# Conditioning rows of a two-block kernel: computed beside the input projection instead of beside the down projection

## The reference

```python
    u = h @ w_in[l]                                   # first block, 60 tiles of 128 columns
    c_q, c_kv, k_r, u_pool, z, xbc, dt, lru_g, lru_x, gates = jnp.split(u, pts, axis=-1)
    y_a = mla_mixer(c_q, c_kv, k_r, cos, sin, ...)    # attention over latents of u
    ...
    x = x + jnp.square(jax.nn.relu(h2 @ w_ff1[l])) @ w_ff2[l]     # up and down projection
...
    mod = (jax.nn.silu(c) @ w_ada[i] + b_ada[i]).reshape(B, N_ADA, D)[:, :, None, :]
    mod_c = (jax.nn.silu(c_ctx) @ w_ada[i] + b_ada[i]).reshape(N_ADA, D)
    hc = _rmsnorm(ctx, norm1_w[i]) * (1.0 + mod_c[1]) + mod_c[0]
    h = _rmsnorm(x, norm1_w[i]) * (1.0 + mod[:, 1]) + mod[:, 0]
```

## Time and profile before

| what | value |
|---|---|
| device time, median of 3 runs | 3533.78 us (3532.81 to 3534.66) |
| device time of the profiled execution | 3534.49 us |
| its span in the profile | 3532.7 us |
| mean granted TensorE clock | 0.987 |
| PE busy | 3403.0 us, 96% |
| DVE busy | 2259.5 us, 64% |
| ACT busy | 1575.2 us, 45% |
| POOL busy | 799.2 us, 23% |
| HBM read, written | 520.67 MB, 103.19 MB |

### The profile page before, as it was taken

The page is one execution under the profiler, slowest core; times in us unless marked ns, Lnnn a source line. Parts: engine busy times, 40 slices in busy tenths (PEclk is TensorE's granted clock), DMA queues, the critical chain, the costliest instruction groups (busy, mean ns, idle before and its releaser), DMA issues.

```text
span 3532.7 us, 43926 instructions
## 1 busy us (share of the span) xinstructions
PE 3403.0 (96%) x17289; PEld 2803.6 (79%) x17289; DVE 2259.5 (64%) x2915; ACT 1575.2 (45%) x1946; POOL 799.2 (23%) x396
## 2 busy tenths in 40 slices
PE   7999999999999999999999999999896999999998
PEld 6667767667878878888888877777775999999997
DVE  4333445645447675666764854545756899999998
ACT  4344443234322343332213433433545677777776
POOL 3111111112212345544431221111222011101112
PEclk9999999999999999999999999999998999999999
DMA  5111113223465323336542241232633999999998
GB/s 201 49 48 54 66 54 103 78 96 131 160 216 184 101 87 117 117 137 223 203 158 71 81 158 65 81 119 98 191 124 151 389 379 378 388 385 385 380 379 311
DMA packets 131725, 626.75 MB, mean 177 GB/s; under 512 B 14849, under 2 KB 15241, under 8 KB 106690
## 3 DMA queue, kind: packets, MB, share of 16 engines
q1 hardware_dynamic: 126626, 606.12, 46.1%
q0 software_dynamic: 4752, 17.30, 1.8%
q10 hardware_dynamic: 144, 0.52, 0.0%
HBM read 520.67 MB, written 103.19 MB: 177 GB/s over the span
## 4 chain that ended last, share of the span: by engine, by line
PE 55%; DVE 6%; ACT 1%; issue 1%; DMA 1%; POOL 0%; POOLq 0%; DVEq 0%; SPq 0%; ACTq 0%
PE bank L268 8%; PE bank L270 7%; PE bank L269 7%; PE bank L3870 5%; PE bank L3869 5%; PE bank L3868 5%; PE bank L2123 3%; PE bank L2125 3%; PE bank L2124 3%; PE bank L3884 2%; PE bank L3885 2%; PE bank L3886 2%; DVE gqJ L2975 1%; PE bank L3855 1%; PE bank L2849 1%
## 5 line engine op out<-in xcount | busy, mean ns | idle before, releaser
L257 POOL TENSOR_TENSOR WL<-WR,WH 128x1024 fp32r<-128x1024 f32 (+1 forms) x177 | 400.6, 2263 | 1721.6 <-ACT WH L249 1718.5
L268 PE MATMUL bank<-XH,WH 128*128 128x512 f32 x1584 | 637.5, 402 | 10.0 <-ACT stg L553 5.0
L270 PE MATMUL bank<-XH,WL 128*128 128x512 f32 x1584 | 617.9, 390 | 0.0
L269 PE MATMUL bank<-XL,WH 128*128 128x512 f32 x1584 | 617.6, 390 | 0.0
L249 ACT ACTIVATE WH<-WR 128x1024 fp32r<-128x1024 f32 (+1 forms) x177 | 173.4, 979 | 511.4 <-PE bank L270 506.3
L3804 DVE TENSOR_TENSOR EL<-ER,EH 128x2816 fp32r<-128x2816 f32 x120 | 371.3, 3100 | 2.2 <-POOL warm L4095 2.2
L268 PEld LDWEIGHTS bank<-XH,WH 128*128 128x128 f32 x1584 | 297.8, 188 | 88.7 <-issue 15.9
L3799 ACT ACTIVATE EH<-ER 128x2816 fp32r<-128x2816 f32 x120 | 307.5, 2563 | 117.2 <-PE bank L3870 84.4
L269 PEld LDWEIGHTS bank<-XL,WH 128*128 128x128 f32 x1584 | 298.1, 188 | 64.7 <-issue 5.0
L270 PEld LDWEIGHTS bank<-XH,WL 128*128 128x128 f32 x1584 | 297.7, 188 | 62.9
L3868 PE MATMUL bank<-EH,WH 128*128 128x352 f32 x1024 | 336.2, 328 | 1.9 <-DVE WL L3992 1.9
(11 more groups left out here) (655 smaller groups left out, 6956.5 us busy)
## 6 DMA issues: line engine op xcount, KB each, us to landing
ER<-in_wu_dram SPq DMA_DIRECT2D x48, 1408.0 KB, 8.6
ER<-in_wd_dram SPq DMA_DIRECT2D x40, 1408.0 KB, 10.9
WR<-in_w_in_dram SPq DMA_DIRECT2D x89, 512.0 KB, 4.4
ER<-in_wg_dram SPq DMA_DIRECT2D x32, 1408.0 KB, 8.5
WR<-in_w_ff_dram SPq DMA_DIRECT2D x64, 512.0 KB, 4.7
aq<-in_w_ada_dram SPq DMA_DIRECT2D x48, 512.0 KB, 3.6
res<-in_wg_dram SPq DMA_DIRECT2D x16, 1408.0 KB, 8.0
res<-in_wu_dram SPq DMA_DIRECT2D x16, 1408.0 KB, 8.3
```

The source lines that it names most:

```text
L257: e.tensor_tensor(lo, raw, hi.bitcast(F32), ALU.subtract).then_inc(*w_lo.up("w_lo", n))
L268: e.matmul(bank[bk][:, 0:b - a], whi, xhi, start=k == 0, stop=False)
L269: e.matmul(bank[bk][:, 0:b - a], whi, xlo, start=False, stop=False)
L270: mm = e.matmul(bank[bk][:, 0:b - a], wlo, xhi, start=False, stop=k == K - 1)
```

## The change

The 48 rows are loaded and reduced between tiles 0 and 5 of the input projection and in the attention's beginning. The diagonals and the broadcast are made right after tile 0, ACT copies the broadcast from PSUM to SBUF (into buffers that the attention uses later), and each row is reduced in whole rows of 1024 with both operands in SBUF. Rows 16 to 47, which the context doesn't need, are done for the latent vector only, so there are 64 such instructions. Rows 0 to 37 rotate through three buffers, rows 38 to 47 through four.

```diff
+    ADA_EARLY, ADA_CHAIN, ADA_LATE = ((0, 3), (3, 7), (7, 11), (11, 15), (15, 22)), ((22, 25), (25, 29), (29, 32)), 38
...
+    def ada_load(e, a):
+        if a >= ADA_LATE + 4:
+            e.wait_ge(*on("ada.ev", a - 4, 0))
+        elif a >= ADA_LATE:
+            e.wait_ge(*(on("mla.qr", 1, 1, 1) if a == ADA_LATE else on("mla.kr")))
+        elif a >= 3:
+            e.wait_ge(*on("ada.ev", a - 3, 1 if a - 3 < 16 else 0))
+        e.dma_start(ada_raw(a), I["w_ada"][a]).then_inc(*d_ada[ada_slot(a)].up("ada", a))
...
+    def ada_pe(e):
+        for i in range(2):
+            e.wait_ge(*on("ada.diag", i))
+            for h in range(2):
+                e.wait_ge(*on.bank(4 + 2 * i + h, "ada.b", i, h))
+                for k in range(4):
+                    o = i * T + (4 * h + k) * 128
+                    mm = e.matmul(bank[4 + 2 * i + h][:, k * 128:k * 128 + 128], ones, ada_diag[:, o:o + 128],
+                                  start=True, stop=True)
+                mm.then_inc(*mla_pe.up("ada.bc", i, h))
+
+    def ada_act(e):
+        for i in range(12, 16):
+            e.wait_ge(*on("p.out", i))
+        for i in range(2):
+            for h in range(2):
+                e.wait_ge(*on("ada.bc", i, h))
+                e.activation(ada_b[i][:, half(h)], bank[4 + 2 * i + h][:, :], AF.Copy).then_inc(
+                    *mla_act.up("ada.b", i, h))
+
+    def ada_diag_dve(e):
+        e.wait_ge(*on("a0.cv"))
+        for i in range(2):
+            for k in range(8):
+                o = i * T + k * 128
+                e.tensor_scalar(ada_diag[:, o:o + 128], ident, cf[:, 2 * k + i:2 * k + i + 1], None,
+                                ALU.mult).then_inc(*mla_dve.up("ada.diag", i))
+
+    def ada_rows(e, a, b):
+        for x in range(a, b):
+            e.wait_ge(*on("ada", x))
+            for i in range(2 if x < 16 else 1):
...
+                e.wait_ge(*mla_dve.now)
+                e.tensor_tensor_reduce(ada_junk, ada_raw(x), ada_b[i], 1.0, pr("b_ada", x), ALU.mult, ALU.add,
+                                       mod[:, x, i:i + 1]).then_inc(*mla_dve.up("ada.ev", x, i))
@@ attention_sp
+        ada_loads(e, 0, 3)
+        for k, (a, b) in enumerate(ADA_EARLY):
+            st.upto("ada", k)
+            ada_loads(e, a + 3, b + 3)
         st.upto("a0")
...
+        st.upto("mla", "ang")
+        ada_loads(e, 25, 28)
+        st.upto("mla", "q")
+        ada_loads(e, 28, 32)
+        st.upto("mla", "kv")
+        ada_loads(e, 32, 39)
+        st.upto("mla", "rope")
+        ada_loads(e, 39, 48)
@@ attention_pe
+        for k in range(5):
+            st.until(2 * k + 2, "ada", k)
+            if k == 0:
+                ada_pe(e)
         st.until(12, "a0")
@@ attention_act, attention_proj_act
+        e.wait_ge(*on("ada.ev", ADA_LATE - 1, 0))
...
+        if i == 0:
+            e.wait_ge(*on("ada.end"))
@@ attention_dve
+        ada_diag_dve(e)
         e.wait_ge(*on("mla.pos_in"))
...
+        for k, (a, b) in enumerate(ADA_EARLY):
+            st.upto("ada", k)
+            ada_rows(e, a, b)
         st.upto("a0")
...
+            ada_rows(e, *ADA_CHAIN[s])
...
+        ada_rows(e, *ADA_CHAIN[2])
...
+                    if n + h < 2:
+                        a = ADA_CHAIN[2][1] + 3 * g + 2 * n + h
+                        ada_rows(e, a, a + 1)
...
+        ada_rows(e, ADA_LATE, 48)
+        on.at["ada.end",] = mla_dve.now
@@ ff_pe_, ff_dve_, ff_sp
-                            mm = e.matmul(bank[4 + 2 * i + h][:, k * 128:k * 128 + 128], ones, (ac2, acq)[i][:, o:o + 128],
...
-                for i in a[2 * h:2 * h + 2]:
-                    ada_dve(e, i)
...
-            for a in ada_of(t):
-                if a + 2 < 48:
-                    ada_load(e, a + 2)
```

More of the change, by code:

```diff
@@ L623, in program, with ada_slot, ada_raw @@
     mla_pe, mla_act, mla_dve = sem("pe_mla"), sem("act_mla"), sem("dve_mla")
+    ADA_EARLY, ADA_CHAIN, ADA_LATE = ((0, 3), (3, 7), (7, 11), (11, 15), (15, 22)), ((22, 25), (25, 29), (29, 32)), 38
+    d_ada = [dma_sem("ada0"), dma_sem("ada1"), d_p, *d_x]
+    ada_b, ada_junk, ada_diag = (qk[:, 3 * T:4 * T], qk[:, 0:T]), qk[:, 2 * T:3 * T], mcs
+    def ada_slot(a):
+        return a % 3 if a < ADA_LATE else 3 + (a - ADA_LATE) % 4
+    def ada_raw(a):
+        return (*(vN[:, k * T:k * T + T] for k in (1, 2, 3)), PT[:, 0:T], tA, cosT, sinT)[ada_slot(a)]
@@ new lines, in ada_load, with ada_loads @@
+    def ada_load(e, a):
[6 more added lines that the diff above has]
+        e.dma_start(ada_raw(a), I["w_ada"][a]).then_inc(*d_ada[ada_slot(a)].up("ada", a))
+    def ada_loads(e, a, b):
+        for x in range(a, b):
+            ada_load(e, x)
+    def ada_pe(e):
[8 more added lines that the diff above has]
+                mm.then_inc(*mla_pe.up("ada.bc", i, h))
@@ new lines, in ada_rows @@
+    def ada_rows(e, a, b):
+        for x in range(a, b):
+            e.wait_ge(*on("ada", x))
+            for i in range(2 if x < 16 else 1):
+                if x == 0:
+                    for k in range(12, 16):
+                        e.wait_ge(*on("p.out", k))
+                    for h in range(2):
+                        e.wait_ge(*on("ada.b", i, h))
+                e.wait_ge(*mla_dve.now)
+                e.tensor_tensor_reduce(ada_junk, ada_raw(x), ada_b[i], 1.0, pr("b_ada", x), ALU.mult, ALU.add,
+                                       mod[:, x, i:i + 1]).then_inc(*mla_dve.up("ada.ev", x, i))
@@ L638, in attention_sp @@
         e.dma_start(D_dt, cqv[32:40, 5 * T:6 * T]).then_inc(*d_dt.up("dt_out"))
-        for x in ("ang", "q", "kv", "rope", "v"):
-            st.upto("mla", x)
+        st.upto("mla", "ang")
[6 more added lines that the diff above has]
+        ada_loads(e, 39, 48)
+        st.upto("mla", "v")
         e.wait_ge(*on("dt_out"))
@@ L761, in attention_act @@
     def attention_act(e, st):
+        st.upto("ada", 0)
+        ada_act(e)
         st.upto("a0")
@@ L1557, in program @@
     d_xin = [dma_sem(f"x_in{i}") for i in range(2)]
-    d_ada = [dma_sem(f"ada{i}") for i in range(2)]
     d_ret = [{x: dma_sem(f"ret{i}{x}") for x in ("q", "qs", "k", "ks", "v", "g")} for i in range(2)]
@@ L2057, in down_at @@
         return range(8 * q + 8 + 2 * m, 8 * q + 10 + 2 * m) if q < 3 and m < 4 else ()
-    def ada_of(t):
-        return range((t - 2) * 48 // 22, (t - 1) * 48 // 22) if 2 <= t < 24 else range(0)
     def up_store(e, n, b):
@@ L2095, in ff_sp @@
             up_store(e, 15, b)
-        for a in range(2):
-            ada_load(e, a)
         for t in range(32):
@@ L2131, in ff_pe_ @@
             q, m = divmod(t, 8)
[L2132 to L2138, removed]
-                            mm = e.matmul(bank[4 + 2 * i + h][:, k * 128:k * 128 + 128], ones, (ac2, acq)[i][:, o:o + 128],
-                                          start=True, stop=True)
-                        mm.then_inc(*ff_pe.up("ada.bc", i, h))
             for h in range(2):
@@ L2262, in ff_dve_ @@
             relu(3)
[L2263 to L2267, removed]
         for t in range(32):
             q, m = divmod(t, 8)
-            a = list(ada_of(t))
             for h in range(2):
-                for i in a[2 * h:2 * h + 2]:
-                    ada_dve(e, i)
                 rs = xc(m)[:, half(h)]
@@ L2285, in ff_dve_ @@
                                    ALU.mult).then_inc(*V.up("cs"))
[L2287 to L2299, removed]
     def ff_pool_(e):
```

3 lines of the change are left out of this document (removed).

## The result

| | before | with the change |
|---|---|---|
| device time, median | 3534.21 us (3532.81 to 3534.66, 4 runs) | 3559.76 us (3557.96 to 3565.06, 4 runs) |
| profiled execution | 3534.49 us | 3558.51 us |
| its span | 3532.7 us | 3556.7 us |

The change makes the kernel slower: the ratio is 1.0075, with a 95% interval from 1.0058 to 1.0093. The profiled execution is 24.0 us longer; the prediction said 24.4 (for the median 3558, measured 3559.76).

The account below looks back on a forecast made before the run. PE, busy for 96% of the span, was taken as the bound. DVE's lateness +25.9, removed broadcast -3.5 and later rows +2 gave +24.4 us: 3558.9 profiled, 3558 for the median, range 3541 to 3568.

Parts of the forecast that it names:

- DVE's arrears: Tiles 1 to 5: DVE falls behind PE, so the first sum of squares starts 25.9 us later, at 157.8.
- the load of tile 9: Attention's beginning: queued behind rows 25 to 27, it lands at 143; 2 us on the path, between 0 and 3.
- The broadcast behind tile 0: After tile 0: PE waits 4.6 us for the diagonals, then half pace; tile 1 starts at 67.6 instead of 57.49.
- The price of one reduction: DVE's reductions of the rows: 1.32 us a pair; 1.27 without the scalar as lower bound.
- What POOL takes: Early rows on DVE: each POOL split, one for each tile, costs DVE up to 2.3 us; lower bound 0.
- DVE against PE: Tiles 1 to 5: a full DVE set takes 13.6 us against PE's 10.88; tile 5's eviction reached at 138.1.
- The later rows: Attention's beginning: 26 rows, one pair each, 34 us of DVE in its gaps; 2 us on the path.
- The last ten rows: Ahead of ACT's first query eviction: they end near 199.5, where it began at 199.18; cost 0, at most 2 us.
- What is removed: Down projection: PE's sixteen broadcast matmuls go, a gain of 3.5 us; DVE's reductions and row loads there give 0.
- POOL not in the way: Rival, chance 0.18: POOL's splits fall into DVE's gaps before tile 5's eviction; +10.8 us, 3545.
- DVE keeping pace: Rival, chance 0.12: DVE's set fits within 10.88 us a tile, so not slower: 3534 us, or 3529.
- the worse case, the clock: Rival, chance 0.10: PE's waits for evictions and ACT also halve its clock, 2.6 us more each; 3565 us.

Follow-up runs that it names:

- thin splits: Changed kernel with POOL subtracting only 8 of the 1024 columns of tiles 3 to 7; 3552.58 us, ratio 1.0053 to the kernel before.
- tile 9 first: Changed kernel with tile 9's load issued ahead of those of rows 25 to 27; 3552.71 us, ratio 1.0058 to the kernel before.

## Why the prediction came out

The mechanisms came out; that the total came so close is luck, because two terms were off in opposite directions: DVE's arrears were put some 5 us too high at the first sum (+20.9 for +25.9), the load of tile 9 some 4.4 too low (6.4 with the half pace behind it, for 2).

- *The broadcast behind tile 0*: right. Wait 4.47 (4.6 predicted), DVE held by POOL's split (the diagonals took 5.31 in place of 3.22), half pace behind. Tile 1 started at 66.50, 1.1 earlier than said, mostly as the broadcast took 5.22 and not 6.15: the half pace held for some 3.5 us of it (twice the 1.7 above full pace) and not 5.3.
- *The price of one reduction*: 1.28 with the scalar, as said, but a pair was 1.33 and 1.44 by turns, mean 1.39, not 1.32: the gap behind the read is 0.04 or some 0.15. In a full set this added less than the shorter stretch took off, 13.33 with the eviction and not 13.6. By the Trainium skill (VectorE: DVE Perf Modes, section on the TRN2 errata) the operation without the scalar would be 1.13, an estimate from the table's row, which the section itself calls too low; the trace, 1.23, does not agree.
- *What POOL takes*: the mechanism is shown (thin splits), the size was 2.0, 2.0, 1.9, 1.9 and 0.9 against "up to 2.3". The Trainium skill, SBUF — State Buffer, section Who interferes with whom, lets such a pair of instructions exclude each other; here the trace agrees for all five splits ahead of the angles. By that section of the Trainium skill the reduction at 79.64 would stand until POOL was through at 81.85, 2.2 us; it lost 2.0. The prediction gave the section without a condition that the Trainium skill makes there: one SBUF input doesn't contend outside the two-port modes. The diagonals, with one SBUF tensor each, did stand (5.31 for 3.22).
- *DVE against PE*: right in kind. Evictions of tiles 1 to 4 ended at 78.40, 93.85, 107.19 and 120.52 (79.2, 95.1, 108.7 and 122.2 predicted), and DVE came to that of tile 5 at 134.02 (138.1). Of the 4.1, 0.8 is tile 1's earlier start, 0.9 the three sets behind it, and 2.4 the last one (0.2 of it a slip in adding, as the parts give 137.9), where the split took 0.9 and not 2.3 and the rows' loads cost 0.68 and 1.10 and not 1.4 twice. This is the first mis-sized term: +25.9 was +21.8 at the eviction and +20.9 at the sum. There PE and DVE were level (the squares were added at 152.3, PE came at 152.81), where I had PE 2 us ahead: its wait of 4.06 for ACT had cost it half pace until 150.3.
- *The later rows*: the load of tile 9 was named, with its place and its mechanism, and taken at 2 us, at most 3. It cost a wait of 4.44 and then 2.0 of half pace. It was asked for when said (158.90, which less the 20.9 is 138.0); the step that failed is that it "lands at 143", 4.5 later: it took 7.2 us from issue to ACT's split, with three rows under way ahead of it and two more transfers behind. Whether the traffic made it slow was not tried apart; that its place in the queue did the harm is shown (tile 9 first). And the half pace behind the wait was put at nothing there. The last ten rows were put at 0 to 2: ACT's first query eviction ended its wait with them, some 0.1 later than with PE alone, and PE had no wait from it: 0.
- *What is removed*: the 3.5 of the broadcast, and nothing of DVE's work there, as said.
- *The rivals*: POOL not in the way is refuted by the thin splits, DVE keeping pace (the second of the list, which the chances call the third) by the evictions. Of the worse case, the clock, half came: pace fell behind the broadcast, which was in the sum, and behind the wait for ACT and the second sum, which were not; it held at the evictions.

## What to carry to other kernels

Work moved from an engine's busy stretch to a freer one gains nothing where the bound engine was already full in the first, and in the second it is the distance between two hand-overs that counts, not the share of free time: here a set and its eviction, 13.3 us or more, stood where PE takes 10.88. What it brings along is costed with it: a broadcast that PE makes in either place can at best be a draw, and each load of the moved work stands in a queue ahead of somebody else's. When two early waits stand before one chain, as the rows' loads and the broadcast here, remove both or neither. And a sum that comes out is no proof of its terms: here two errors of 5.0 and 4.4 us hid each other.

## What was not expected of the hardware

- All five stretched reductions ended 1.08 us behind the POOL instruction that they met (for instance 79.64 + 3.29 = 82.93, and 78.85 + 3.00 = 81.85), as did the one of before, wherever they began. A reduction that DVE had begun first held POOL instead: each of the five splits took 2.26 us and what was left of the reduction under way (78.85: 0.74 left of 78.32 + 1.27, and 3.00 long; 89.74: 0.16 left of 88.62 + 1.28, and 2.42 long).
- PE went to half pace behind waits of 4.06, 4.44 and 4.47 us and not behind 2.14 and 2.16, nor behind 3.17 with the diagonals early (79.90, granted clock 1.00 from 80 to 83); in between lie the 3.04 (full pace) and 3.87 (half pace) of the earlier trace rows.
- A load of 512 KB took about twice as long among five others: 7.1 and 9.4 us to landing for the two loads of tiles from 150 to 170 us, where the median of before was 3.5 from 50 to 130 us and 4.3 from 130 to 170.
